# A 16-byte tensor allocated ahead of the others in a two-block network kernel

## The reference

```python
def conv_glu_ffn(h, w_gate, w_up, conv_w, w_down):
    gate = causal_dwconv(h @ w_gate, conv_w)
    return (jax.nn.gelu(gate, approximate=True) * (h @ w_up)) @ w_down

for l in range(DEPTH):                       # DEPTH = 2
    h = rms_norm(x, pre_mix_g[l])
    z = h @ w_in[l]
    ...
    x = x + rms_norm(mix, post_mix_g[l])
    h = rms_norm(x, pre_ffn_g[l])
    y = conv_glu_ffn(h, ffn_w_gate[l], ffn_w_up[l], ffn_conv_w[l], ffn_w_down[l])
    x = x + rms_norm(y, post_ffn_g[l])
```

## Time and profile before

| | before |
|---|---|
| median of three runs | 2313.12 us (2312.5 to 2313.26) |
| the profiled execution | 2319.24 us |
| its span | 2317.5 us |
| TensorE busy | 2195.9 us, 95% |
| VectorE busy | 1209.4 us, 52% |
| ScalarE busy | 899.5 us, 39% |
| mean granted TensorE clock | 0.976 |

### The profile page before, as it was taken

How to read it: one execution, slowest core, us unless ns; L and a number is a source line. 1 busy time by engine, 2 the same in 40 slices (tenths; PEclk the granted TensorE clock), 3 DMA queues, 4 the chain that set the end, 5 groups by cost and what they waited for, 6 DMA issues and landing times. The chain is left out here.

```text
span 2317.5 us, 35396 instructions
## 1 busy us (share of the span) xinstructions
PE 2195.9 (95%) x14540; PEld 1556.2 (67%) x14540; DVE 1209.4 (52%) x2075; ACT 899.5 (39%) x1611; POOL 45.7 (2%) x36
## 2 busy tenths in 40 slices
PE   7999999899999999989998999999999988999998
PEld 4774454588888767744446888886777566886546
DVE  5553344666662275443546666524528775443554
ACT  5423234433333354133344333333336554323462
POOL 2000001000000020000010000000000000000000
PEclk9999999999999999999999999999999989999999
DMA  5201111122222221011112222222221102222000
GB/s 196 73 3 42 52 56 37 55 91 97 104 83 100 91 73 55 22 37 56 38 37 73 91 96 105 91 91 96 93 91 55 37 19 91 91 91 74 36 1 37
DMA packets 23920, 159.79 MB, mean 69 GB/s; under 512 B 3024, under 2 KB 3664, under 8 KB 4944
## 3 DMA queue, kind: packets, MB, share of 16 engines
q1 hardware_dynamic: 23760, 157.53, 19.2%
HBM read 155.43 MB, written 2.10 MB: 68 GB/s over the span
## 5 line engine op out<-in xcount | busy, mean ns | idle before, releaser
L673 DVE TENSOR_TENSOR arena_r<-ring,arena_r 128x512 fp32r<-128x512 f32 x448 | 313.2, 706 | 473.4 <-ACT arena_r L664 468.6
L664 ACT ACTIVATE arena_r<-ring 128x512 fp32r<-128x512 f32 x448 | 279.4, 631 | 613.3 <-PE banks L714 582.7
L712 PE MATMUL banks<-oT_r,arena_r 128*128 128x512 f32 x1104 | 457.4, 414 | 12.6 <-DVE arena_r L673 8.7
L714 PE MATMUL banks<-oT_r,arena_r 128*128 128x512 f32 x1104 | 439.6, 398 | 0.0
L713 PE MATMUL banks<-hT_r,arena_r 128*128 128x512 f32 x928 | 368.9, 398 | 0.0
L713 PE MATMUL banks<-arena_r,arena_r 128*128 128x512 f32 x704 | 277.1, 394 | 0.0
L712 PEld LDWEIGHTS banks<-oT_r,arena_r 128*128 128x128 f32 x1104 | 209.5, 190 | 77.2 <-DVE arena_r L944 12.5
L712 PE MATMUL banks<-arena_r,arena_r 128*128 128x512 f32 x592 | 239.9, 405 | 15.1 <-DVE arena_r L704 10.9
L714 PEld LDWEIGHTS banks<-oT_r,arena_r 128*128 128x128 f32 x1104 | 208.9, 189 | 50.7
L714 PE MATMUL banks<-arena_r,arena_r 128*128 128x512 f32 x592 | 232.6, 393 | 0.0
L713 PEld LDWEIGHTS banks<-hT_r,arena_r 128*128 128x128 f32 x928 | 176.1, 190 | 46.5 <-issue 7.2
(11 more groups left out here) (387 smaller groups left out, 2929.6 us busy)
## 6 DMA issues: line engine op xcount, KB each, us to landing
ring<-weights SPq DMA_DIRECT2D x142, 1024.0 KB, 4.8
xT<-x_features SPq DMA_DIRECT2D x2, 1024.0 KB, 6.2
arena<-memory SPq DMA_DIRECT2D x2, 1024.0 KB, 5.0
y_features<-xT SPq DMA_DIRECT2D x8, 256.0 KB, 2.0
const<-constants SPq DMA_DIRECT2D x1, 1088.0 KB, 15.6
const<-constants SPq DMA_DIRECT2D x1, 512.0 KB, 16.4
arena<-positions SPq DMA_DIRECT2D x1, 256.0 KB, 2.6
small<-small_vectors SPq DMA_DIRECT2D x2, 68.5 KB, 6.3
```

Of the source, the lines that this page charges most:

```text
L664: act.activation(hi, self.stream.block(b, n), ACT.Copy).then_inc(self.chip.sem("hi_ready"), 1)
L673: vec.tensor_tensor(lo[:, 0:n * P], self.stream.block(b, n), hi[:, 0:n * P].bitcast(F32), ALU.subtract).then_inc(self.chip.sem("lo_ready"), 1)
L712: pe.matmul(out, w_hi, hi, start=k == 0, stop=False)
L714: ins = pe.matmul(out, w_lo, hi, start=False, stop=k == nk - 1)
```

## The change

A tensor of four columns, `lbc`, which used to be allocated behind `lbt`, is allocated first. Nothing else is edited.

```diff
+        self.lbc = sb("lbc", 4)
         self.ring = sb("ring", RING * SLOT_BLOCKS * P)
         self.xT = sb("xT", KD * S)
         self.hT = sb("hT", KD * S)
...
         self.lbt = sb("lbt", 4 * DEPTH)
-        self.lbc = sb("lbc", 4)
         self.arena = sb("arena", ARENA * S)
```

## The result

| | before | after |
|---|---|---|
| median of four runs | 2312.81 us (2311.16 to 2313.26) | 2294.89 us (2292.07 to 2296.39) |
| ratio, 95% interval | | 0.9922 (0.9906 to 0.9937) |
| the profiled execution | 2319.24 us | 2292.07 us |
| its span | 2317.5 us | 2290.3 us |

The change makes the kernel faster by 0.78%, 17.9 us (interval 14.6 to 21.7). The forecast was 2291.5 us.

The account below looks back on a forecast made before the run. TensorE, busy 2195.9 of 2317.5 us, was taken as the bound. Terms -22 + 0.3 = -21.7 us took the profiled 2319.2 to 2297.5; the runs' median being 6.1 lower gave 2291.4, stated as 2291.5 us, range 2286 to 2309.

Parts of the forecast that it names:

- What bounds the kernel: Whole kernel: TensorE has little slack; 1280 float32r triples with an operand in `hT` or `oT` pay 20 ns each.
- Where the 20 ns come from: Float32r triples: an operand at a multiple of 64 bytes costs, 700 ns against 680 with all 32 behind.
- down slower than 1.36 us: Down stage, two triples: named as a sign of being wrong, that the relation counts and not the start.
- The page's fixed cost: Back-to-back matmuls at full clock: about 2.5 ns each, 215.7 ns for 512 columns; by it the change would give nothing.
- One operand is enough for the full price: Float32r triples: a single operand at a multiple of 64 already brings (nearly) the full 700 ns.
- Term 1: The 1280 triples with an operand in `hT` or `oT` come to 680 ns: -22 us, ends -18 and -25.6.
- Terms 2, 3 and 5: Float32 products from `ring`: 0; VectorE and ScalarE: 0, at most -1 us; `small`, `lbt`, `lbc` read in columns: 0.
- Term 5: `small`, `lbt` and `lbc`, read in columns of a few elements: 0.
- Term 4: DMAs: at the start the last big constant lands later, +0.3 us, ends 0 and +0.7; weights have ample cover.
- The slower case: DMA writes beginning at half of 64 bytes are slow, some 2470 us at a factor of 2.5; chance 0.03.
- the one of half the effect: Triples: 20 ns made of two parts, the 32-byte step and other bits or moving-tile/weights relation; 2302 us, chance 0.13.
- The rival of the other bits: Starts of `hT`, `oT` against `arena`: not the 32-byte step but perhaps the bit worth 256; no change, 2313, chance 0.15.

Follow-up runs that it names:

- e2: Kernel before with `lbc` allocated between `xT` and `hT`, so `ring` and `xT` stay at a multiple of 64: 2294.21 us, ratio 0.9917.
- e3: Kernel before with `lbc` allocated between `hT` and `oT`, so `oT` and `const` go 32 bytes behind a multiple of 64: 2301.84 us, ratio 0.9956.
- e5: Kernel before with 224 bytes ahead of `arena`, all at multiples of 64, `hT`, `oT` and `arena` alike by 256: 2294.66 us, ratio 0.9911.
- e6: Kernel before with 96 bytes ahead of `arena`, all at multiples of 64, alike by 128 but not by 256: 2307.37 us, ratio 0.9971.
- e1: Kernel before with 32 bytes more ahead of `arena`, so that it too begins at a multiple of 64: 2311.39 us, ratio 0.9995.
- e4: Changed kernel with 32 bytes more ahead of `arena`, which then begins at a multiple of 64: 2311.82 us, ratio to before 1.0001.
- the bench: No network, only TensorE: rows of back-to-back matmuls, operand starts and types varied; float32r 233.3 ns with moving tile at 32, weights at 0, 226.9 both at 32.
- the sweep: No network, only TensorE: rows of 48 float32r matmuls, moving tile's start stepped by 16 bytes, shapes varied; 226.7 to 227.7 ns at distance 0.

## Why the prediction came out right, step by step

- **What bounds the kernel**, that 1280 triples pay 20 ns each at the full clock, and that this pace sets the time: shown. After the change the stages of 1168 of them have 680 ns and the two short ones with an operand in `hT` 686 and 687, TensorE has no new wait, and where the experiments move the pace (e2, e3, e5, e6) the time moves with it, where they leave it (e1, e4) the time stays.
- **Where the 20 ns come from**: this step failed, though the number rests on its right half. It said that an operand at a multiple of 64 costs. e1 (down at 680 with all at multiples of 64), e5 (the whole gain so) and e4 (no gain with `oT` and `hT` 32 behind) show that for tensors at multiples of 32 it is the distance of moving and stationary operand that counts, by 256. I read "all operands 32 behind" as the cause, where the same rows said "all alike". The change makes both true at once, so that the number was lucky in this step; with the pad of e4 the same reasoning would have given gate and up 680 ns, and they took 700. One sign that the prediction named, down slower than 1.36 us if the relation counts, could not appear: down has all its operands in `arena`, alike before and after. The page's fixed cost of 2.5 ns for each matmul ("TensorE: Matmul & The Clock Gate" of the Trainium skill, section "Wait — 56ns, not 53.3ns?") is what the bench has for bfloat16 (215.8 ns) and for each record of float32 (429.2 = 2 x 213.3 + 2.5); for float32r of 512 columns it does not hold, 226.7 to 236.5 ns here.
- **One operand is enough for the full price**: only partly. The earlier trace rows had 700 ns with one unlike matmul of three, e3 and the bench have 693.4 and 693.6 with one of three at the same distance. What makes the difference was not tried, and its cause stays open.
- **Term 1**, -22 us: counted matmul by matmul, for all of the affected triples whose next start comes within 245 ns, the excess over 226.7 ns each was 23.6 us before and is 3.0 us after, so 20.6 us are saved. The 3.0 us are left in the first eight steps of the stages and between attention's work. Part of it is a start-up that the bench shows by itself: in the row `mg,wa`, at distance 0, the first ten or so matmuls follow each other at 224 to 236 ns before the row settles at 226.7.
- **A term left out**: 576 float32r matmuls of 256 columns (L2540 to L2542), for which being alike is the dearer case. Followed from start to start their middle value rose from 117 and 118 to 120 ns, about +1.3 us, as in the sweep. The total of the mechanism is then -19.3 us, well inside the measured 14.6 to 21.7.
- **Terms 2, 3 and 5**: float32 products indifferent (in the bench, and L748 keeps its 592 ns in the kernel), VectorE's lo part unchanged at 706. The additions of L938 went from 684 to 690 ns, 0.2 us in all. Term 5 was not looked at by itself.
- **Term 4**, +0.3 us for DMAs: the weights land in 4.7 us and the last big constant in 16.4 as before, so 0. The slower case had nothing to start from. The 16-byte lines of "SBUF — State Buffer", section "Door 1: The DMA port swizzle", of the Trainium skill don't give what the runs show: every start here is a multiple of 16, and a period of 256 bytes decides, as e5 and e6 show.
- **The rivals**: the one of half the effect named the true cause in passing, "the relation of moving tile and weights", but gave it half of the 20 ns, where it has all of them. The rival of the other bits was right that bits above the one worth 32 matter, since those worth 64 and 128 do (e1, e6). The one worth 256, which it named, does not: it still differs after the change.

The two profiled executions differ by 27.2 us, more than the medians. Their mean granted clock was 0.976 and 0.980, and the runs of one kernel spread by 2 to 12 us; I read nothing into the remainder.

## What to carry to other kernels

Where float32r matmuls of 512 columns set the time, give the moving and the stationary tensors starts that are multiples of 32 and alike by 256 bytes; it costs some padding and took 3% off each such matmul (233.3 to 226.7 ns). This was measured for 128 columns of weights; another shape can have another best distance and has to be measured. Keep it under watch: a small tensor allocated anywhere ahead shifts all the others, and can take 0.8% of a kernel away or bring it. When two stages of one instruction shape run at two paces, list what differs in their operands, and try relation and place apart before believing either.

## What was not expected of the hardware

- The pace of back-to-back float32r matmuls depends on the distance of the two operands in a partition, with a period of 256 bytes, from 226.7 to 234.6 ns in the sweep; bfloat16 and float32 do not. At half the clock it doesn't either (427 ns before and after the change).
- Starts at 16 or 48 bytes can break this rule: 233.3 ns with both operands at 48, 227.3 with 16 against 48, 236.5 with 16 against 32.
- In a triple the prices don't add up: one matmul of three at a distance of -32 cost 13 to 20 ns, where the curve would give 7.
- The cheap distance depends on the shape: 0 for 128 columns of weights and 512 moving, 32 (and not 0) for 96 columns, and with 256 moving columns 0 and 96 are the dear ones (119.8 and 119.7 ns against 117.8 to 118.7).
- Even at the best distance a float32r matmul of 512 columns takes 11 ns more than a bfloat16 one, 226.7 against 215.8, and fewer columns of weights don't take it away (231.5 and 232.9 with 32). What it is was not found out.
